# The seams between the stages of a two-layer trunk, cut into three blocks of 352 tokens

## What is computed

```
layer 0: x += (B * conv3(C * V)) @ w_sc_out     with B, C, V = rmsnorm(x) @ w_sc_in
         x += (silu(conv3(g) + b) * u) @ w_down with g, u = rmsnorm(x) @ w_up       (d_ff 2816)
layer 1: x += stick_breaking(q, k, v) @ w_o     with q, k, v = rmsnorm(x) @ w_qkv  (16 heads; samples also read 256 cached keys)
         x += the same FFN with its own weights
y = rmsnorm(x)
rmsnorm(x) = x * rsqrt(mean(x * x) + 1e-6) * g
```

## Time and profile before

| | |
|---|---|
| median of 3 runs | 2736.73 us (2732.05 to 2737.2) |
| the profiled execution | 2740.34 us, span 2738.3 us |
| PE busy | 2612.5 us (95%) |
| DVE busy | 1450.5 us (53%) |
| ACT busy | 508.7 us (19%) |
| POOL busy | 715.5 us (26%) |
| chain that ended last | PE 88%, DVE 7%, issue 2%, ACT 2%, DMA 1% |
| mean granted clock of TensorE | 0.983 |

### The profile page before, as it was taken

The page is one execution under the profiler, slowest core; times in us unless marked ns, Lnnn a source line. Parts: engine busy times, 40 slices in busy tenths (PEclk is TensorE's granted clock), DMA queues, the critical chain, the costliest instruction groups (busy, mean ns, idle before and its releaser), DMA issues.

```text
span 2738.3 us, 40374 instructions
## 1 busy us (share of the span) xinstructions
PE 2612.5 (95%) x16774; PEld 2474.4 (90%) x16774; DVE 1450.5 (53%) x1328; ACT 508.7 (19%) x905; POOL 715.5 (26%) x405
## 2 busy tenths in 40 slices
PE   6999999999999999988999999789999999999995
PEld 6999999999999999977888888559899999999995
DVE  6333436444444444466777777633654444444446
ACT  3000112000000000124444444420200000000012
POOL 3333323322233332321111111002323222333332
PEclk9999999999999999999999999999999999999997
DMA  3111111111111111131111111631111111111111
GB/s 128 47 47 47 41 46 46 41 46 47 47 47 47 40 46 39 50 110 39 40 40 40 40 47 40 206 120 47 39 39 47 47 47 47 47 47 47 47 42 63
DMA packets 58213, 149.00 MB, mean 54 GB/s; under 512 B 5458, under 2 KB 25682, under 8 KB 58066
## 3 DMA queue, kind: packets, MB, share of 16 engines
q1 hardware_dynamic: 49186, 122.42, 13.8%
q10 hardware_dynamic: 8880, 24.29, 2.3%
HBM read 128.91 MB, written 17.78 MB: 54 GB/s over the span
## 4 chain that ended last, share of the span: by engine, by line
PE 88%; DVE 7%; issue 2%; ACT 2%; DMA 1%; SPq 0%; DVEq 0%; ACTq 0%
PE bank L442 26%; PE bank L446 26%; PE bank L445 25%; PE bank L615 3%; PE bank L555 3%; PE bank L588 2%; DVE h_lo L1062 1%; DVE x L1160 1%; DVE y L1150 1%; ACT a_hi L744 1%; DVE total L1072 1%; DVE h_lo L1108 1%; PE bank L453 1%; PE bank L558 0%; PE bank L678 0%
## 5 line engine op out<-in xcount | busy, mean ns | idle before, releaser
L442 PE MATMUL bank<-h_hi,w_hi 128*128 128x352 f32 x3648 | 1195.5, 328 | 40.2 <-DVE h_lo L1062 21.7
L446 PE MATMUL bank<-h_hi,w_lo 128*128 128x352 f32 x3648 | 1179.4, 323 | 0.0
L445 PE MATMUL bank<-h_lo,w_hi 128*128 128x352 f32 x3648 | 1175.5, 322 | 0.0
L442 PEld LDWEIGHTS bank<-h_hi,w_hi 128*128 128x128 f32 x3648 | 688.1, 189 | 56.6 <-issue 36.6
L416 POOL CAST w_hi<-raw 128x1024 fp32r<-128x1024 f32 x196 | 212.5, 1084 | 1960.9 <-PE bank L442 1914.1
L445 PEld LDWEIGHTS bank<-h_lo,w_hi 128*128 128x128 f32 x3648 | 692.7, 190 | 0.0
L446 PEld LDWEIGHTS bank<-h_hi,w_lo 128*128 128x128 f32 x3648 | 688.7, 189 | 0.0
L418 POOL TENSOR_TENSOR w_lo<-raw,w_hi 128x1024 fp32r<-128x1024 f32 x196 | 493.2, 2517 | 15.7
L1160 DVE TENSOR_TENSOR x<-x,bank 128x1056 f32<-128x1056 f32 x192 | 238.8, 1251 | 319.1 <-PE bank L446 319.1
L442 PE MATMUL bank<-a_hi,w_hi 128*128 128x352 f32 x1056 | 343.4, 325 | 8.5 <-DVE x L1160 8.5
L445 PE MATMUL bank<-a_lo,w_hi 128*128 128x352 f32 x1056 | 341.5, 323 | 0.0
(11 more groups left out here) (104 smaller groups left out, 1654.3 us busy)
## 6 DMA issues: line engine op xcount, KB each, us to landing
raw<-weights SPq DMA_DIRECT2D x196, 512.0 KB, 3.4
page_k<-cache_k SPq DMA_DIRECT2D x16, 512.0 KB, 7.0
page_v<-cache_v SPq DMA_DIRECT2D x16, 512.0 KB, 6.3
x_spill<-x ACTq DMA_DIRECT2D x8, 528.0 KB, 6.4
k_out<-k_t ACTq DMA_DIRECT2D x8, 528.0 KB, 2.7
v_out<-v_t ACTq DMA_DIRECT2D x8, 528.0 KB, 2.7
x<-x_spill ACTq DMA_DIRECT2D x8, 528.0 KB, 7.4
y_out<-y_rows ACTq DMA_DIRECT2D x3, 1408.0 KB, 5.2
```

The lines of the kernel that those rows point to most:

```text
L442: mm = nc.tensor.matmul(o, w_hi[w][:, c0:c0 + P], hi, start=first, stop=False)
L445: nc.tensor.matmul(o, w_hi[w][:, c0:c0 + P], lo, start=False, stop=False)
L446: return nc.tensor.matmul(o, w_lo[w][:, c0:c0 + P], hi, start=False, stop=last)
```

## The change

All seams are cut in blocks of 352 tokens.

- Load of x: the first block of each chunk first, one DMA per chunk; then blocks 1 and 2 in two DMAs each on SyncE's queue, with the load of weight tile 1 between them.
- The first tile of a stage (`first_linear`) goes over the blocks outside and the input chunks inside, and waits for each chunk of each block. The last tile of sc_in, sc_out and wo (`last_linear`) does the same and signals each block (`block_full`).
- The last group of each FFN (`last_down`) makes 24 blocks of six matmuls in a ring of seven banks; VectorE adds each into x and frees it (`block_taken`). It waits at its start for both results of the group before.
- High parts, low parts, squares, sums, roots and reciprocals are made per block. ScalarE and VectorE split block by block as soon as block_full comes. Before qkv, splits of all blocks come first and then the squares; in the last norm squares and sums go with the adds.
- The means go to bank[2]. At norm 0 all three follow tile 1; at norms 1 and 3 two follow tile 0 and the third follows tile 1. At norm 2 they follow the second, third and fourth piece of k and q. In ffn1's last group two of the last norm's means stand between its blocks.
- The nine first pieces of qkv use six banks rather than two, and VectorE weighs the first head before it takes the last two pieces.
- The final products: GpSimd has all eight of blocks 0 and 1, VectorE five of block 2.

```diff
-Y_BY_DVE = 5
+Y_BY_DVE = (0, 0, 5)
+RING, MEAN_BANK = 7, 7
+FIRST_BANK = [3, 4, 5, 2, 0, 1, 2, 0, 1]
+MEANS_IN = ((), (KC * 2 - 2, BLOCKS - 4))
...
             for f in range(1, KC, 2):
-                sp.dma_start(x[:, f, :], x_in[f, :, :]).then_inc(x_loaded[f], 16)
-            load_tile(1, 1)
+                sp.dma_start(x[:, f, tokens(0)], x_in[f, :, tokens(0)]).then_inc(x_loaded[f], 16)
+            for j in range(1, TJ):
+                for g in range(2):
+                    rows = slice(g * KC // 2, (g + 1) * KC // 2)
+                    sp.dma_start(x[:, rows, tokens(j)],
+                                 x_in[rows, :, tokens(j)].rearrange("f p t -> p f t")).then_inc(x_rest[j - 1][g], 16)
+                if j == 1:
+                    load_tile(1, 1)
...
+            def mean_of(nth, j, n):
+                pe.wait_ge(summed, summed_by(nth, j))
+                nc.tensor.matmul(projected(n), mean[:, :], total[:, tokens(j)], start=True, stop=True).then_inc(mean_full, 1)
+            def means(nth):
+                for j in range(2):
+                    mean_of(nth, j, 6 + j)
+            def last_mean(nth):
+                pe.wait_ge(root_made, TJ * nth + 1)
+                mean_of(nth, 2, 6)
...
+            def first_linear(tile, s, fill, h_base):
+                pe.wait_ge(w_split, tile + (RAW + 1))
+                pe.wait_ge(taken[s], fill + 1)
+                for j in range(TJ):
+                    for k in range(KC):
+                        pe.wait_ge(h_ready, h_base + j * KC + k + 1)
+                        mm = three(out[s][:, j, 0:TW], tile % SPLIT, k * P, h_hi[:, k, tokens(j)],
+                                   h_lo[:, k, tokens(j)], k == 0, k == KC - 1, k == j == 0)
+                mm.then_inc(full[s], 1)
...
             def up(tile, ring0, k0, name, trip, h_base=None, norm=None):
...
+                    if n == 0 and h_base is not None:
+                        first_linear(tile, s, fill, h_base)
+                        means(norm)
+                    else:
+                        linear(tile + n, (ring0 + n) % SPLIT, s, fill)
+                    if n == 1 and norm is not None:
+                        last_mean(norm)
...
+            def last_down(tile, name_after, group, base, nth, mean_after):
+                for kk in range(2):
+                    pe.wait_ge(w_split, tile + (RAW + 1 + kk))
+                    pe.wait_ge(a_ready, group * 2 + (3 + kk))
+                for s in range(2):
+                    pe.wait_ge(taken[s], FREE[name_after][s] + 1)
+                for c in range(BLOCKS):
+                    j, f = c // KC, c % KC
+                    if c >= RING:
+                        pe.wait_ge(block_taken, base + c - RING + 1)
+                    for kk in range(2):
+                        mm = three(projected(c % RING), (tile + kk) % SPLIT, f * P, a_hi[:, 0, kk, tokens(j)],
+                                   a_lo[:, 0, kk, tokens(j)], kk == 0, kk == 1,
+                                   (c, kk) in ((0, 0), (BLOCKS - 1, 1)))
+                    mm.then_inc(block_full, 1)
+                    if c in mean_after:
+                        mean_next(nth, mean_after.index(c))
...
             for n in range(CHUNKS):
-                if n >= 2:
-                    pe.wait_ge(lin_taken, n - 1)
-                project(first, n, n % 2, None, H_QKV if n == 0 else None)
+                if n < 6:
+                    pe.wait_ge(block_taken, TAKEN_FFN0 + BLOCKS - RING + (FIRST_BANK[n] - 3) % RING + 1)
+                else:
+                    pe.wait_ge(lin_taken, n - 3 + 1)
+                project(first, n, FIRST_BANK[n], None, H_QKV if n < TJ else None)
+                if 1 <= n <= TJ:
+                    mean_next(2, n - 1)
...
+            def norm_of_ffn():
+                for c in range(BLOCKS + 1):
+                    if c < BLOCKS:
+                        add_block(B_FFN0, c)
+                    if c:
+                        low(2, (c - 1) % KC, (c - 1) // KC)
+                for j in range(TJ):
+                    for f in range(KC):
+                        sum_block(2, f, j, KC * j + f)
+                    if j:
+                        invert(2, j - 1)
+            def final_norm():
+                for c in range(BLOCKS + 1):
+                    if c < BLOCKS:
+                        add_block(B_FFN1, c)
+                    if c:
+                        sum_block(4, (c - 1) % KC, (c - 1) // KC, c - 1)
+                    if c == 2 * KC + 2:
+                        invert(4, 0)
+                for j in range(1, TJ):
+                    invert(4, j)
```

More of the change, by code:

```diff
@@ L260, in projected, with tokens @@
         def projected(n):
-            return out[0][:, n, 0:TW]
+            return bank[n // 3][:, n % 3, 0:TW]
+        def tokens(j):
+            return slice(j * TW, (j + 1) * TW)
         turned = [out[0][:, 2, :], out[1][:, 2, :]]
@@ L428, in _ @@
             for j in range(TJ):
[L429 to L434, removed]
+                pool.wait_ge(rstd_made, TJ * 4 + j + 1)
+                for f in range(Y_BY_DVE[j], KC):
+                    pool.wait_ge(y_gained, KC * j + f + 1)
+                    nc.gpsimd.tensor_tensor(y_rows[:, f, tokens(j)], y_rows[:, f, tokens(j)], rstd[:, tokens(j)],
                                             ALU.mult).then_inc(y_by_pool, 1)
@@ L446, in three, with linear @@
                 return nc.tensor.matmul(o, w_lo[w][:, c0:c0 + P], hi, start=False, stop=last)
[L448 to L457, removed]
+            def mean_of(nth, j, n):
[7 more added lines that the diff above has]
+                mean_of(nth, 2, 6)
+            def linear(tile, ring, s, fill):
                 pe.wait_ge(w_split, tile + (RAW + 1))
@@ L484, in up @@
                     s = (k0 + n + 1) % 2
[L485 to L489, removed]
+                    fill = trip * TRIP_FILLS + (FREE[name][s] + (k0 + n) // 2)
+                    if n == 0 and h_base is not None:
[5 more added lines that the diff above has]
+                        last_mean(norm)
             def down(tile, ring0, k0, name, trip, slot, group, early_release):
@@ L527, in ffn, with sc_in @@
                 last = 4 + 6 * (PAIRS - 1)
-                down(t0 + last, t0 + last, 4 + (4 + KC) * (PAIRS - 1), name, 0, 0, g0 + PAIRS - 1, False)
+                last_down(t0 + last, ("wo", "end")[layer], g0 + PAIRS - 1, (TAKEN_FFN0, TAKEN_FFN1)[layer], (2, 4)[layer],
+                          MEANS_IN[layer])
             pe.wait_ge(made, 1)
-            def sc_in(trip, first):
+            def sc_in(trip):
                 for n in range(6):
                     s = (n + 1) % 2
[L536 to L543, removed]
+                    tile, fill = trip * 6 + n, trip * 3 + (FREE["sc_in"][s] + n // 2)
+                    if tile == 0:
+                        first_linear(tile, s, fill, H_SC_IN)
+                    elif tile == N_SC_IN - 1:
+                        last_linear(tile, s, fill)
+                    else:
+                        linear(tile, n % SPLIT, s, fill)
+                    if tile == 1:
+                        means(0)
+                        last_mean(0)
+            for i in range(KC // 2):
+                sc_in(i)
             tiles_of("sc_out", T_SC_OUT, H_SC_OUT)
@@ L1096, in norm @@
[L1096 to L1108 removed]
+                f, added = KC - 1, TJ * (nth // 2)
```

403 lines of the change are left out of this document (228 added, 175 removed).

## The result

The median fell from 2736.01 us (four runs, 2732.05 to 2737.2) to 2711.51 us (four runs, 2709.24 to 2713.09): ratio 0.991, 95% interval 0.9897 to 0.9924. That is 24.5 us faster. The direction was right and the time lies in the range, but two thirds of the 36 us of the forecast came. The profiled execution took 2711.09 us; its span is 29.0 us shorter than that of before.

What follows compares the result with a forecast made beforehand. TensorE, busy nine tenths or more nearly everywhere, loses time at seams waiting for VectorE's whole 1056-token chunks. Terms 8+4+1-3+12+5+1+8 = 36 us, taken from the 2736.7 median, give 2700.7; 80% between 2684 and 2716.

Steps and rivals of the forecast that it cites:

- qkv: From ffn0 to qkv: splits behind each down block let qkv start at once; gain 12 us (8 to 15).
- norm 0: At the start: tile 1 covers the sums, tile 2 starts at 46; gain 8 us, lower end 3.
- the first attention step: TensorE stood 6.91 us for v_rows; the first weighing now lies ahead of two takes; gain 5 us (0 to 7).
- sc_out: From sc_in to sc_out: 5.2 us lost before, 1.2 lost to GpSimd's subtraction after; gain 4 us (2 to 5).
- the two FFN seams: sc_out to ffn0 and wo to ffn1: 6.5 to 8.1 us lost against 8.5; gain 1 together (0 to 4).
- the last down groups: At their start TensorE waits for both banks of the group before; cost 1.5 us each, 3 together.
- the 5 us chain: Before tile 2 of ffn0 and ffn1: third mean, root, reciprocal and product stand open, 5.1 us.
- Tail: Final norm: adds, squares and sums run beside the matmuls, GpSimd ends the kernel; gain 8 us (2 to 11).
- (a): Rival: each seam finds VectorE free of GpSimd and TensorE warm; gain 46 to 55 us, near 2686; chance 0.2.
- (b): Rival: cover fails at norm 0 and tail, open reciprocal chains leave TensorE cold; gain 12 to 25 us; chance 0.2.
- (c): Rival: slower, GpSimd's subtractions hold VectorE's small two-input operations one by one, 0.72 us more each; chance 0.03.
- (d): Rival: some whole-chunk wait remains, so blocks are not separated; 2733 to 2737 us; chance 0.02.

Runs made afterwards that it cites:

- the cut pair: GpSimd's subtraction for w_lo cut from 1024 to 32 columns, in the kernel before (2710.77 us) and in the kernel after (2679.35 us).
- the run with other final products: Against the kernel after, VectorE takes three final products of block 1 and six of block 2, rather than none and five: 2703.24 us.

## Why the forecast was right, and where it was too high

The time lies in the range and the mechanisms were mostly right. But the terms missed by up to 5.8 us, two that were too high (qkv, norm 0) and one that was too low (the first attention step), and these errors partly cancel: in so far the agreement is luck.

**Which stalls go, and what is late next: right.** sc_out, the two FFN seams, the last down groups and wo came within 0.9 us of their terms. The third mean costs what the cut of that seam saves; its removal gave 11.6 us. The wait of 1.5 us and the 5 us chain were there to a few tenths, and GpSimd ended the kernel.

**qkv: the term of 12 us was mis-sized; it measured 6.2.** The forecast left 8.3 us of the 20.3 open; 14.1 stayed (37.4 less six pieces of 3.86 and 0.16). The step that failed is "two GpSimd subtractions then meet the sums", at 2.4 each. The traces show three whole splits, casts included: 4.7 us of hold ahead of the first sums and 2.8 in the third block's, 7.5 together. TensorE's waits for the sums were 4.4, 0 and 3.2 us, where the forecast had 2.3, 0.5 and 2.9. Then came cold stretches of 3.85 us at 0.50 and 5.67 at 0.70, which cost 1.9 and 1.7 us, where I had "some cold". With the subtractions cut the same seam gains 12.9.

**Norm 0: 4.5 instead of 8.** Tile 2 started at 45.7, where the working said 46, and before's tile 2 at 53.4 or 51.9. The working gave 5 us; I raised it to 8 for the case that GpSimd misses VectorE. It didn't in any of eight executions, with the load early or late: the hold only changes place. Even without the subtractions it is 6.3.

**First attention step: 8.4 instead of 5.** The wait for v_rows was 6.9 and is now 0.63 us, so I took too little of it. The rest is clock. From the tenth piece to the thirteenth, in before and in after (columns as in the earlier trace rows):

```profile
1244.45:1281.10 36.65, 29.75 (x228) 24.64 (x226) 28.30 (x26) 13.21 (x19) 5.98 (x2) 0.86 0.06 19
```
```profile
1224.27:1252.22 27.95, 27.32 (x228) 22.35 (x226) 24.10 (x24) 12.99 (x19) 4.15 (x2) 1.00 0.08 26
```

The same 228 matmuls keep TensorE busy for 2.4 us less; the forecast had no term for that.

**Tail: 7.4 instead of 8**, with the order of events as forecast. GpSimd's products took 1.20 us beside VectorE, as assumed, and 0.92 where I had 0.85, for which no row stood.

**The range.** The high ends of the terms add to 53.5 us, not 55; it changes nothing here.

**The rivals.** (a), a gain of 46 to 55, needed seams free of GpSimd. That is not this kernel; even the cut pair differs by 31.4 us in the medians and 35.5 in the profiled spans. (b), cold clock and failed cover, had the size right (24.5 lies in its 12 to 25 and not in my 26 to 45) and the cause in part: cold at ffn0, qkv and ffn1, but not a failing tail. (c), every small operation held: refuted by the median of 0.574 us of 96 splits in after (0.577 with the subtractions cut); a few are held, up to 2.72 us. One subtraction holds one operation, however small, so cutting chunks in three does not multiply the hold. (d) did not happen.

The Trainium skill (SBUF — State Buffer, "SBUF: two separate sides") has the lock bind VectorE operations with two SBUF inputs or in a two-port mode, and the other engine block for the whole instruction. The traces agree, also in what is not held (next section). They add that the wait isn't over with one instruction of the other engine: GpSimd's cast took 7.59 us while VectorE ran one split behind another.

The Trainium skill's advice of 512 elements or more (VectorE: DVE Perf Modes, section on the trn2 errata) spoke against the change. VectorE's busy time did grow, by 25 us with the holds in it; how much of that lay on the path no run separates, but the seams gained in spite of it.

## What to carry to other kernels

Cutting a seam into blocks moves the wait to the first thing that still needs all blocks: look for it (here one mean, placed one tile too late, cost 11.6 us) and put it where its chain is covered. When two engines hinder each other, count every instruction of the one that starts inside the other's chain, casts too, since the cost goes by the number that meet; moving the load only moved the hold. A wait of TensorE of 3.2 to 4.4 us cost about half as much again in cold clock here (1.6 to 2.8 us).

## What the hardware showed

- What GpSimd holds, from the operations' minimum, median and maximum in ns. Sums of 1056 in sc_out and wo take 2530 to 2537, and 1258 to 1260 with the subtractions cut: twice as long. The copy of one SBUF input is held too (279/336/2522). Adds that read PSUM and one SBUF operand are never held (one of 1.25 us at 1144.99 in after ran beside a subtraction that began at 1144.96), nor are reciprocals (two took 4.71 us beside GpSimd's final products):

```profile
L1169 DVE RECIPROCAL rstd<-total x15: 2294/2345/2354, 42.8 to 2691.3; 128x352 f32<-128x352 f32 x15
L1196 DVE TENSOR_TENSOR total<-total,square x12: 2530/2532/2537, 327.0 to 1895.3; 128x1056 f32<-128x1056 f32 x12
L1161 DVE COPY total<-square x9: 279/336/2522, 25.7 to 2677.9; 128x352 f32<-128x352 f32 x9
```
```profile
L1160 DVE TENSOR_TENSOR x<-x,bank x192: 1240/1254/1257, 325.5 to 2703.9; 128x1056 f32<-128x1056 f32 x192
```

  The first block is of after, the second of before.
- The hold goes both ways: GpSimd's cast, 1.04 us alone, took 3.09 at 13.84 in norm 0 of after, among VectorE's splits, and 7.59 at 13.61 in the run with other final products.
- TensorE's clock after an idle: 2.27 us left it at 1.00 (2.4 GHz); 4.4 us were followed by 0.50 (1.2 GHz) for 4 us, and 3.2 us by 5.67 us of which the first part was at 0.50 (0.70 on the mean). The length alone doesn't decide: in before an idle of 2.79 us at sc_out left it at 1.00, and one of 2.71 at ffn0 was followed by 0.50 (0.59 on the mean from 408.81 to 413.00).
- The same code differs by up to 5.7 us in one stage from execution to execution (114.5 to 120.2 in the samples).
